# A fused two-layer decoder step on one core: order of the set-up loads, place of the first unit's rotation tables, place of the raw state-space inputs

## What is computed

```
shift, scale, gate = adaln(c, w_mod, b_mod, 3)            # silu(c) @ w_mod + b_mod, 9 rows of c
h = modulate(rms_norm(x, norm_pre), shift, scale)
u = h times B, group by group                             # 64 groups of 16 channels, 64 states each
s_t = a * s_(t-1) + u_t      (complex, associative scan)  # a = exp(lam * dt)
y = Re(C s) + d_skip * h
out = gelu(y) * sigmoid(gelu(y) @ w_glu + b_glu)
```

## Time and profile before

| what | value |
|---|---|
| median of the runs shown | 1191.7 us (1191.6 to 1192.0) |
| the profiled execution's own time | 1190.8 us |
| its span, first to last instruction | 1189.1 us |
| busy PE, DVE, ACT, POOL | 1074.2, 810.7, 560.3, 249.4 us (90, 68, 47, 21%) |
| granted TensorE clock, mean over the span | 0.946 |
| moved by DMA | 205.0 MB, mean 172 GB/s |

### The profile page before, as it was taken

How to read it: one execution, slowest core, us unless ns; L and a number is a source line. 1 busy time by engine, 2 the same in 40 slices (tenths; PEclk the granted TensorE clock), 3 DMA queues, 4 the chain that set the end, 5 groups by cost and what they waited for, 6 DMA issues and landing times.

```text
span 1189.1 us, 19332 instructions
## 1 busy us (share of the span) xinstructions
PE 1074.2 (90%) x6916; PEld 707.8 (60%) x6916; DVE 810.7 (68%) x1311; ACT 560.3 (47%) x1146; POOL 249.4 (21%) x392
## 2 busy tenths in 40 slices
PE   3789999999979999999879997889989699999995
PEld 0456565665636666666546765546666366666663
DVE  5699895988587777744572567765544777777434
ACT  2421121122556666654462427754445476666542
POOL 1385554560001122100010122013410021111000
PEclk9789989999989999999989997889999799999998
DMA  8667768777733444244602530017882133343441
GB/s 347 242 216 242 279 236 339 276 247 289 328 142 130 154 142 142 99 147 146 239 1 91 204 134 19 1 62 240 273 309 101 63 142 143 142 147 113 144 143 45
DMA packets 52531, 205.04 MB, mean 172 GB/s; under 512 B 7250, under 2 KB 36050, under 8 KB 41810
## 3 DMA queue, kind: packets, MB, share of 16 engines
q1 hardware_dynamic: 49362, 195.40, 45.5%
q0 software_dynamic: 3072, 8.39, 2.3%
HBM read 199.39 MB, written 4.38 MB: 171 GB/s over the span
## 4 chain that ended last, share of the span: by engine, by line
PE 76%; DVE 12%; ACT 4%; DMA 3%; issue 2%; SPq 2%; POOL 1%; DVEq 0%; ACTq 0%; POOLq 0%
PE PS L488 17%; PE PS L487 16%; PE PS L491 15%; PE PS L647 7%; DVE space L1447 4%; PE PS L885 4%; PE PS L504 3%; PE PS L515 2%; PE PS L676 2%; DVE wk_sb L1447 2%; DMA x_sb<-x 2%; DVE rinv L1451 1%; PE PS L817 1%; PE PS L802 1%; PE PS L838 1%
## 5 line engine op out<-in xcount | busy, mean ns | idle before, releaser
L487 PE MATMUL PS<-space_rounded 128*128 128x320 f32 x1344 | 565.8, 421 | 27.3 <-DVE space L1447 20.8
L488 PE MATMUL PS<-space_rounded,lo 128*128 128x320 bf16 x1344 | 427.4, 318 | 0.0
L491 PE MATMUL PS<-space,ring 128*128 128x320 bf16 x1344 | 402.7, 300 | 0.0
L1447 DVE TENSOR_TENSOR lo<-ring,space_rounded 128x1024 bf16<-128x1024 f32 (+1 forms) x172 | 205.7, 1200 | 214.1 <-ACT space_rounded L987 212.4
L487 PEld LDWEIGHTS PS<-space_rounded 128*128 128x128 f32 x1344 | 255.4, 190 | 95.3 <-DVE space L1447 26.7
L987 ACT ACTIVATE space_rounded<-ring 128x1024 fp32r<-128x1024 f32 (+1 forms) x172 | 176.6, 1032 | 222.9 <-PE PS L488 219.9
L488 PEld LDWEIGHTS PS<-space_rounded,lo 128*128 128x128 bf16 x1344 | 129.4, 96 | 125.0 <-issue 3.5
L491 PEld LDWEIGHTS PS<-space,ring 128*128 128x128 bf16 x1344 | 135.5, 101 | 0.0
L647 PE MATMUL PS<-space 128*128 128x256 f32 x512 | 115.6, 384 | 0.0
L647 PEld LDWEIGHTS PS<-space 128*128 128x128 f32 x512 | 96.6, 191 | 28.9 <-issue 16.3
L1550 DVE SCALAR_TENSOR_TENSOR space<-space,vec_sb 128x336 f32<-128x336 f32 x176 | 91.6, 565 | 1.9 <-ACT space L1029 0.6
(11 more groups left out here) (220 smaller groups left out, 1374.3 us busy)
## 6 DMA issues: line engine op xcount, KB each, us to landing
ring<-w_mod SPq DMA_DIRECT2D x22, 2048.0 KB, 8.8
ring<-w_up SPq DMA_DIRECT2D x22, 2048.0 KB, 8.0
ring<-w_down SPq DMA_DIRECT2D x16, 1408.0 KB, 6.0
space<-pool_cmp SPq DMA_DIRECT2D x128, 128.0 KB, 2.3
ring<-w_mod_kv SPq DMA_DIRECT2D x4, 2048.0 KB, 10.2
ring<-w_kv SPq DMA_DIRECT2D x3, 2048.0 KB, 8.1
ring<-w_glu SPq DMA_DIRECT2D x2, 2048.0 KB, 8.0
space<-w_mod SPq DMA_DIRECT2D x2, 2048.0 KB, 16.7
```

Of the source, the lines that this page charges most:

```text
L487: pe.matmul(out, wr[:, p % SPLIT, at:at + P], xr[:, k, :], start=start, stop=False)
L488: mm = pe.matmul(out, lo[:, p % SPLIT, at:at + P], xh[:, k, :], start=False, stop=False)
L491: return pe.matmul(out, w, xl[:, k, :], start=False, stop=stop)
L1447: return dve.tensor_tensor(out, a, b, op)
```

## The change

SP now issues `lam` and `log_dt` first, then the constants (with a semaphore of their own, `consts_in`), and only then waits for the memset and issues `c`; `x` follows at once, ahead of one modulation chunk; then `braw`, `craw`, `h0`, `vec`, the page table and two more chunks. ACT makes `dt` and `mag` first, then `silc`, and squares `x` before the sines. PE starts with `sums(0)`, and the transposes of `BX` stand ahead of `modulation(3)`. `braw` and `craw` move to the arrays of the scan (`zf`, `decay`), so unit 0's pages wait for nothing on DVE; ACT instead waits for `cx_done` before it overwrites `decay`. Unit 0's tables are made into `vc` (which receives its values in unit 8 and later) and POOL makes them as soon as the sines are there; its wait for `hs` and `scaled` moves to unit 1. DVE scales `h` before it turns the modulation over, and the weighting is folded into `turned_modulation`. Nothing of the computation is left out.

The helper lines (`V`-views, renamed arguments of `cosine`, `sine`, `sine_of`) are cut:

```diff
+        first_tables = vc[...][:, 0:4 * T].rearrange("p (q i t) -> p q i t", q=2, i=2)
+        def cos_table(u):
+            return first_tables[:, 0] if u == 0 else TC[:, u % 2]
+        def sin_table(u):
+            return first_tables[:, 1] if u == 0 else TS[:, u % 2]
-        braw = XT[:, 0]...[:, 0:1024]...
-        craw = XT[:, 0]...[:, 1024:2048]...
+        braw = zf[:, 0:1024]...
+        craw = decay[:, 0:1024]...
 # SP
-            sp.wait_ge(S("c_zero"), 1)
-            sp.dma_start(silc[:, :, 0:NB], dram["c"]).then_inc(S("c_in"), 16)
             sp.dma_start(lam, ...).then_inc(S("params_in"), 16)
             for e in range(2):
                 sp.dma_start(ldt[64 * e:64 * e + 64, :], ...).then_inc(S("params_in"), 16)
-            sp.dma_start(consts[:, :], dram["consts"]).then_inc(S("params_in"), 16)
-            sp.dma_start(pages[:, :], dram["page_table"]).then_inc(S("pages_in"), 16)
-            for n in range(RING):
-                chunk(stream[n][0])
-            sp.dma_start(vec[:, :], dram["vec"]).then_inc(S("vec_in"), 16)
+            sp.dma_start(consts[:, :], dram["consts"]).then_inc(S("consts_in"), 16)
+            sp.wait_ge(S("c_zero"), 1)
+            sp.dma_start(silc[:, :, 0:NB], dram["c"]).then_inc(S("c_in"), 16)
+            sp.dma_start(x, dram["x"]).then_inc(S("x_in"), 16)
+            chunk("mod0")
             sp.dma_start(braw, ...)   # craw, h0 likewise, all on bc_in
-            sp.dma_start(x, dram["x"]).then_inc(S("x_in"), 16)
+            sp.dma_start(vec[:, :], dram["vec"]).then_inc(S("bc_in"), 16)
+            sp.dma_start(pages[:, :], dram["page_table"]).then_inc(S("pages_in"), 16)
+            chunk("mod1")
+            chunk("mod2")
             for n in range(RING, NMOD0):
                 chunk(stream[n][0])
             sp.dma_start(w1, ...)
-            for j in mod_of_unit[0]:
-                chunk(f"mod{j}")
...
-                if u < 2:
+                if u == 1:
                     sp.wait_ge(S("bt_mm"), 4)
-                    sp.wait_ge(S("cx_done"), 1)
...
-                if 1 <= u < DB:
+                if u < DB:
                     for j in mod_of_unit[u]:
                         chunk(f"mod{j}")
 # PE
             pe.wait_ge(S("silc"), 1)
+            pe.wait_ge(S("consts_in"), 16)
+            sums(0)
             for j in range(NMOD0 - 1):
                 modulation(j)
-            sums(0)
-            modulation(NMOD0 - 1)
             pe.wait_ge(S("bx_done"), 4)
...
+            modulation(NMOD0 - 1)
 # ACT
-            act.wait_ge(S("c_in"), 16)
-            act.activation(silc, silc, ACT.Silu).then_inc(S("silc"), 1)
-            act.wait_ge(S("params_in"), 64)
+            act.wait_ge(S("params_in"), 48)
             act.activation(pr["dt"], ldt, ACT.Exp).then_inc(S("dt"), 1)
             act.wait_ge(S("lrdt"), 1)
             act.activation(pr["mag"], pr["lrdt"], ACT.Exp).then_inc(S("mag"), 1)
+            act.wait_ge(S("c_in"), 16)
+            act.activation(silc, silc, ACT.Silu).then_inc(S("silc"), 1)
+            squares(x, "x_in", 16, 0)
             act.wait_ge(S("phases"), 2)
...
-            act.wait_ge(S("vec_in"), 16)
-            squares(x, "x_in", 16, 0)
             root(0)
-            wide(0)
...
+            wide(0)
+            act.wait_ge(S("mod_ev"), 1)
+            modulated(0, 0)
             page_bias(0)
-            modulated(0, 0)
+            act.wait_ge(S("cx_done"), 1)
 # POOL
             pool.wait_ge(S("trig"), 2)
             pool.wait_ge(S("mag"), 1)
-            pool.wait_ge(S("hs"), 1)
-            pool.wait_ge(S("scaled"), KT)
...
-                if u >= 2:
+                if u == 1:
+                    pool.wait_ge(S("hs"), 1)
+                    pool.wait_ge(S("scaled"), KT)
+                elif u >= 2:
                     pool.wait_ge(S("s_ready"), u - 1)
 # DVE
-            dve.wait_ge(S("params_in"), 64)
+            dve.wait_ge(S("params_in"), 48)
...
+            dve.wait_ge(S("consts_in"), 16)      # ahead of the phases
...
-            dve.wait_ge(S("bc_in"), 48)
+            dve.wait_ge(S("bc_in"), 64)
...
-            post(dve.tensor_copy(rinv[:, 0:1], AH[:, 0, 0, 0:1]), "cx_done")   # now posted by the last AH
             inverse(0)
-            turned_modulation(0)
-            norm_weights(0, g_pre[:, 0], None)
-            modulated(0, 0, None)
+            for k in range(KT):
+                post(tt(h[:, k, 0:SEQ], x[:, k, 0:SEQ], rinv[:, 0:SEQ], ALU.mult), "scaled", own=False)
+            link(tt(h[:, :, SEQ:T], x[:, :, SEQ:T], rinv[:, SEQ:T]..., ALU.mult))
+            turned_modulation(0, g_pre[:, 0])    # with norm_weights inside, ahead of mod_ev
+            link(tt(samples(h), samples(h), per_sample(8), ALU.mult))
+            post(tt(samples(h), samples(h), per_sample(0), ALU.add), "hs")
+            dve.wait_ge(S("scaled"), KT)
```

More of the change, by code:

```diff
@@ L1345, in grid @@
                     return v.rearrange("p (i a b) -> p i a b", i=2, a=16)
-                for tabl, (x1, x2), (y1, y2), op in ((TC, (0, 0), (1, 1), ALU.subtract), (TS, (1, 0), (0, 1), ALU.add)):
+                for tabl, (x1, x2), (y1, y2), op in ((cos_table(u), (0, 0), (1, 1), ALU.subtract), (sin_table(u), (1, 0), (0, 1), ALU.add)):
                     pool.tensor_tensor(grid(pt1), fine(x1), coarse(x2), ALU.mult).then_inc(S("pool_chain"), 1)
@@ L1351, in _ @@
                     pool.wait_ge(S("pool_chain"), n_tab[0])
-                    tab(pool.tensor_tensor(tabl[:, s, :, 0:SEQ], pt1.rearrange("p (i t) -> p i t", i=2),
+                    tab(pool.tensor_tensor(tabl[:, :, 0:SEQ], pt1.rearrange("p (i t) -> p i t", i=2),
                                            pt2.rearrange("p (i t) -> p i t", i=2), op))
-                    pool.tensor_copy(tabl[:, s, :, SEQ:T].rearrange("p i (b t) -> p i b t", b=DB),
-                                     tabl[:, s, :, 0:DS].unsqueeze(2).broadcast_to([P, 2, DB, DS])).then_inc(S("tables"), 1)
+                    pool.tensor_copy(tabl[:, :, SEQ:T].rearrange("p i (b t) -> p i b t", b=DB),
+                                     tabl[:, :, 0:DS].unsqueeze(2).broadcast_to([P, 2, DB, DS])).then_inc(S("tables"), 1)
                 if u >= 1:
@@ L1667, in turned_modulation, with cosine, sine @@
                 tile = mod_tile[n]
-                post(tt(mod[:, tile:tile + 16, :], turned_of(n).rearrange("p (m b) -> p m b", b=32)[:, :, 0:NB],
-                        b_mod[:, tile:tile + 16].unsqueeze(2).broadcast_to([P, 16, NB]), ALU.add), "mod_ev")
-            turned_modulation(0)
+                ins = tt(mod[:, tile:tile + 16, :], turned_of(n).rearrange("p (m b) -> p m b", b=32)[:, :, 0:NB],
+                         b_mod[:, tile:tile + 16].unsqueeze(2).broadcast_to([P, 16, NB]), ALU.add)
+                if norm is not None:
+                    link(ins)
+                    sc_ = mod[:, tile + 8:tile + 16, :]
+                    ins = dve.scalar_tensor_tensor(out=sc_, in0=sc_, scalar=1.0, in1=norm.unsqueeze(2).broadcast_to([P, KT, NB]),
+                                                   op0=ALU.add, op1=ALU.mult)
+                post(ins, "mod_ev")
             g_pre = V["norm_pre"].rearrange("p (s k) -> p s k", s=4)
             g_post = V["norm_post"].rearrange("p (s k) -> p s k", s=4)
-            norm_weights(0, g_pre[:, 0], None)
-            modulated(0, 0, None)
-            def cosine(s):
-                return TC[:, s].unsqueeze(2).broadcast_to([P, 2, 2, T])
-            def sine(s):
-                return TS[:, s].unsqueeze(2).broadcast_to([P, 2, 2, T])
+            for k in range(KT):
+                post(tt(h[:, k, 0:SEQ], x[:, k, 0:SEQ], rinv[:, 0:SEQ], ALU.mult), "scaled", own=False)
+            link(tt(h[:, :, SEQ:T], x[:, :, SEQ:T], rinv[:, SEQ:T].unsqueeze(1).broadcast_to([P, KT, DB * DS]), ALU.mult))
+            turned_modulation(0, g_pre[:, 0])
+            link(tt(samples(h), samples(h), per_sample(8), ALU.mult))
+            post(tt(samples(h), samples(h), per_sample(0), ALU.add), "hs")
+            dve.wait_ge(S("scaled"), KT)
+            def cosine(u):
+                return cos_table(u).unsqueeze(2).broadcast_to([P, 2, 2, T])
+            def sine(u):
+                return sin_table(u).unsqueeze(2).broadcast_to([P, 2, 2, T])
             def y_read(f):
@@ L1696, in hidden_sum, with sine_of @@
                 post(tt(out[:, 0:7, :, 7], out[:, 0:7, :, 7], far[:, 1:8, :, 0], ALU.add), "hid_sum", own=False)
-            def sine_of(t2, z, s):
-                link(tt(t2[:, :, 0, :], z[:, :, 0, :], TS[:, s], ALU.mult))
-                return dve.scalar_tensor_tensor(out=t2[:, :, 1, :], in0=z[:, :, 1, :], scalar=-1.0, in1=TS[:, s], op0=ALU.mult, op1=ALU.mult)
+            def sine_of(t2, z, u):
+                link(tt(t2[:, :, 0, :], z[:, :, 0, :], sin_table(u), ALU.mult))
+                return dve.scalar_tensor_tensor(out=t2[:, :, 1, :], in0=z[:, :, 1, :], scalar=-1.0, in1=sin_table(u), op0=ALU.mult, op1=ALU.mult)
             for u in range(units):
```

(8 more changed lines are left out.)

16 lines of the change are left out of this document (10 added, 6 removed).

## The result

| | before | changed |
|---|---|---|
| median of 18 runs each, same sessions | 1191.36 us | 1187.72 us (1184.25 to 1192.82) |
| the profiled execution | 1190.8 us | 1185.5 us |
| its span | 1189.1 us | 1183.7 us |
| mean granted clock | 0.946 | 0.949 |

The ratio is 0.9972, 95% interval 0.9961 to 0.9983: 3.3 us faster (2.0 to 4.6). Run again beside other kernels, the same kernel gave 0.9952 (0.9936 to 0.9969), 5.7 us (3.7 to 7.6). The forecast was 5.2 us, 1186.5: the first interval leaves the 5.2 out, the second takes it in.

The account below looks back on a forecast made before the run. PE carries three quarters of the chain; tables and pages hold the unit loop back. A 5.2 us lead, kept to the end, takes 1190.8 to 1185.6, plus 0.9 for the median: 1186.5 us, range 1181.2 to 1190.4.

Parts of the forecast that it names:

- Parameters and phases: Set-up: parameters issued about 1.15 us sooner, DVE starts near 6.2, phases at 8.2 (3.3 us early), sines to 20.8.
- x at 11.1 to 12.5: Set-up: x, behind only c, lands then; squares and table load end at 16.8, hidden with 1.9 us to spare.
- POOL beside DVE: Set-up behind the sines: POOL's tables and DVE's 15 small instructions exclude each other; DVE loses 5.1 us.
- The count of ten instructions in POOL's pass: Set-up: ten of DVE's 15 small instructions fit into POOL's 7.5 us, where they take 2.4.
- the bound of 0 for this term: Set-up: lower bound of DVE's loss beside POOL, if they don't meet; the upper is 7.5 us, POOL first throughout.
- BX at 29.5, reciprocal at 39.9, hs at 48.5, DVE's unit 0 at 51.2, unit 0's compression until 62.0: DVE's chain to h and unit 0: BX later than before, DVE's unit 0 4.5 us sooner, compression ending 62.0 against 64.2.
- Unit 0 without POOL's company: Unit 0: POOL's tables for unit 1 are over before DVE's scan, so it costs DVE 11.2 us, not 12.9.
- The chunk for unit 2 at 79.2: Unit loop: chunk lands 17.2 us after unit 0's compression; unit 2's compression ends at 88.4 instead of 93.6, lead 5.2.
- I let 5.2 us stand to the end: Unit loop: the 5.2 us lead lasts, since everything later waits for what PE or DVE did, not for a time.
- the engines don't meet: Rival, set-up: POOL and DVE run side by side, hs at 43.4, lead 10, time 1181.6 us; chance 0.15.
- POOL wins every turn: Rival, set-up: DVE loses 7.5 us, and 1.1 as constants come no sooner; lead 1.7, 1190.0 us; chance 0.18.
- x among the crowd: Rival, set-up: x shares the wire with chunk and raw inputs, lands as late as 26.8, up to 1198.9 us; chance 0.08.

Follow-up runs that it names:

- experiment 2: Changed kernel with x loaded behind the second and third modulation chunk, squares behind the sines again: ratio 0.9954, median 1185.7 us.
- experiment 1: Changed kernel with POOL waiting for h before unit 0's tables instead of before unit 1's: ratio 0.9955, median 1186.2 us.
- experiment 4: Changed kernel with SP issuing a unit's modulation chunk ahead of its pages from unit 2 on: ratio 0.9939, median 1183.9 us.
- experiment 7: Kernel before, with a unit's modulation chunk issued ahead of its pages from unit 2 on: ratio 1.0005, median 1191.6 us.
- Experiment 9: Changed kernel with chunk ahead of pages, plus DVE adding the compression halves ahead of turned_modulation and y_read: ratio 0.9894, median 1178.5 us.
- experiment 11: Kernel before, with only unit 0's tables made early in vc, without POOL's wait for h: ratio 1.0009, median 1191.4 us.
- 3: Changed kernel with raw inputs again in the place of unit 0's pages and the fifth chunk ahead of the pages: ratio 0.9968, median 1187.5 us.

## Why the prediction was right

Most steps came out within 0.4 us.

- Parameters and phases: DVE at 6.2, phases at 8.2, sines done at 20.8 were forecast; 6.14, 8.19 and 20.79 measured.
- x at 11.1 to 12.5, measured 11.77; hidden, as forecast, and even where it came at 30.6 (experiment 2).
- POOL beside DVE: 5.1 us forecast from one scan and one copy, 5.1 measured as the difference of 8.66 and 3.56, and shown to be POOL's doing by experiment 1, where moving POOL away gave it back. The Trainium skill's rule ("SBUF — State Buffer", "Who interferes with whom"), by which a VectorE instruction with two SBUF inputs contends with a GpSimd instruction that reads SBUF, holds for 32 columns as for 1280. One reading was wrong: I let one of the 15 pass for its single input, but two have a single input, and the `TENSOR_SCALAR` waited as long as the others (1.14 us instead of 0.18). The count of ten instructions in POOL's pass came out even so (20.79 to 28.00). And the bound of 0 for this term had a row against it, the one at 60.37.
- BX at 29.5, reciprocal at 39.9, hs at 48.5, DVE's unit 0 at 51.2, unit 0's compression until 62.0: measured 29.48, 39.85, 48.2, 51.03 and 61.91.
- Unit 0 without POOL's company: 11.2 us forecast, 10.97 measured (51.03 to 62.00).
- The chunk for unit 2 at 79.2: PE took it at 79.54. I named it as what limits the lead, and experiment 4 showed that it was, through the change alone (7). The compression of unit 2 ended at 89.86, not 88.4, since after 3.46 us of idleness the modulation took 3.22 us at a granted clock of 0.58 (79.5 to 82.7), not the 1.92 us that it takes where 1.00 is granted (121.7 to 123.6).
- "I let 5.2 us stand to the end": the lead dipped to 3.5 in unit 4 and was 5.8 from unit 6 on. The step came out in size, and partly by luck. I had compared the changed kernel's ring of chunk and pages with PE's own time, and had not seen that DVE holds PE in unit 5 in both kernels. There the dip was given back: the kernel before stood idle for 2.03 us and ran the modulation behind it in 3.25 us (granted clock 0.58), the changed one 1.38 and 1.92 (1.00). That is 0.65 and 1.33 us, 2.0 of the 5.8, and neither stood in the prediction. Experiment 9 took that wait away.
- The measured 3.3 us of the first comparison (2.0 to 4.6) lie below the 5.2, the 5.7 of the second above. The two profiled executions of the changed kernel agree: leads of 5.8 and 5.5 us, times of 1185.5 and 1185.6. The executions that make the first median 2.2 us higher have no profile. Within the first session the clock goes with the time (0.943: 1190.5 to 1192.8; 0.949 and 0.950: 1184.3 to 1187.8), and for one pair of profiles experiment 7 shows slower products in the same code. But the clock does not explain the two medians: the mean clock of the runs is the same in both sessions (0.9465 and 0.9467), and a run at 0.944 took 1185.8 in the second and 1186.8 and 1188.5 in the first. Why they differ stays open.

The rival "the engines don't meet" is refuted by the chain of waits and by experiment 1; "POOL wins every turn" by 5.1 instead of 7.5 and, for its other half, by the phases at 8.19; "x among the crowd" by 11.77.

## What to carry to other kernels

A wait of 7.8 us for tables was worth nothing when it alone was removed (experiment 11), and a load that ends the longest chain was worth nothing when it was put back (2). The gain came from parameters, tables and pages together: parameters alone left 1.3 us of lead, tables alone 0.5, and taking back the early tables or the free pages cost 1.4 and 1.5 of the 5.8 (1, 3); the pages alone were not run. Several paths of nearly the same length met in unit 0. Moving a GpSimd pass under VectorE's work is not free where both read SBUF through two inputs: for a VectorE chain of small dependent instructions, charge the length of the GpSimd pass less the few that get in between (7.5 - 2.4 us here). In a loop in which two engines hand work to each other, put first on each what the other waits for: one reordered line gave about as much lead as the whole change (5.8 us each), on top of it.

## What had not been expected of the hardware

A chain of dependent 32-column VectorE instructions (0.20 us each alone) beside eight GpSimd instructions of 0.3 to 1.3 us advanced by about one instruction per GpSimd instruction, and GpSimd was hardly held up: its pass took 7.5 us as alone. The loss falls on the engine with the short instructions. A long one of VectorE (the scan) makes GpSimd pay as well: its copy took 2.70 us instead of 0.29, while the scan took 3.92 instead of 2.86. And a `TENSOR_SCALAR` over 32 columns, with one SBUF input, was held up like those with two (1.14 us instead of 0.18), while a reciprocal with one was not (0.35).

Two executions of which the loop agreed to 0.1 us differed by 6.8 us at the end, with the granted clock 0.01 lower between 290 and 950 us.
